# The last five tiles of a weight matrix are loaded in two DMAs of unequal numbers of partitions

## The chip, the cores and the metric

The kernel runs on one core of one Trainium2 chip. The metric is the device time of one execution in microseconds (us), as the median of several runs. The core has the engines PE (TensorE, matrix products), DVE (VectorE), ACT (ScalarE), POOL (GpSimd) and SP (SyncE, which here only issues DMAs), and 16 DMA engines that all DMAs of the core share.

## What is computed

One layer of a diffusion backbone over 512 latent tokens of width 1024 with 256 context tokens. First comes a token mixer (a bidirectional state-space scan and a gated short convolution between two projections), then an expert-retrieval mixer. The second part holds most of the time. Cut to what matters:

```python
q = (xb @ w_q).reshape(T, PEER_HEADS, 2, PEER_HALF)          # w_q: 1024 x 2048
s = jnp.einsum('thpd,hpnd->thpn', q, keys)
sv, si = lax.top_k(s, PEER_TOPK)                             # 16 of 128, per head and side
cand = (sv[:, :, 0, :, None] + sv[:, :, 1, None, :]).reshape(...)
cv, ci = lax.top_k(cand, PEER_TOPK)                          # 16 experts for each of 8 heads
eid = i1 * PEER_N_KEYS + i2                                  # which expert rows
g = jax.nn.softmax(cv, axis=-1)
u = jnp.take(u_tab, eid, axis=0)
act = jax.nn.gelu(jnp.einsum('thkd,td->thk', u, xb))
return jnp.einsum('thk,thkd->td', g * act, jnp.take(v_tab, eid, axis=0))
```

Each token fetches 8 x 16 = 128 rows of u and v. They lie side by side in one table, so that a row is 2048 numbers of 4 bytes, 8 KB.

## The kernel before

Tokens lie on the 128 partitions, in four tiles. For each tile there are 128 gathers: one gather fetches, for every one of the 128 tokens of the tile, the row of one of its experts, 128 rows of 8 KB. That makes 512 gathers, numbered 0 to 511, all issued by POOL at L766 as indirect DMAs. They land in slots of SBUF of 8 KB per partition. The number of slots changes over the program, between 6 and 11, since slots come and go with the memory that other stages free. A gather waits until the gather that used its slot before is consumed.

Of each row, DVE multiplies the u half with the token and sums (L1960). ACT makes the gate (L1423, L1428). The v half times its gate is added up either by DVE (L1977) or by PE with a diagonal matrix that ACT makes (L1436, L1133). Two gathers are handled as a pair. After the last pair of a token tile ACT copies PE's sums out (L1443), and DVE adds, normalises and adds the residual (L1988 to L1999). SP stores the tile (L637).

Scores for later tiles are computed in the same time: PE multiplies the tokens with `w_q` (L1076), transposes (L1086), multiplies with the keys (L1095), and DVE ranks.

All large weights come in tiles of 128 partitions x 2048 numbers (8 KB per partition, 1 MB) through a ring of four buffers, `wring`. SP issues their loads in one written order, the list `loads`; load n goes into buffer n % 4, after the last user of load n - 4 is through. Each buffer has a semaphore, to which every load adds 16 when it has landed, and PE waits for the right multiple of 16 in `weights(n)`. The tiles of `w_q` are loaded twice, eight for token tiles 0 and 1, and from `wq_0[1]` on eight more for token tiles 2 and 3. These last eight are the last weights of the program. Here they are called tile 0 to tile 7. PE's products take them in pairs (0, 1), (2, 3), (4, 5), (6, 7), each pair for two token tiles.

SP's list holds 92 DMAs in all: 1 of 128 rows of vectors, 80 weight tiles with 128 rows of 8 KB each, 6 token tiles of 128 rows, 1 that loads 256 rows of tokens again and 4 stores of 128 rows. ACT issues eight: one of 104 rows (`rows_b`), the dt weights and three vectors spread over 128 partitions (4 x 128), one store of 32 rows (`row_scratch`) and two loads that spread those over 128 partitions (2 x 128).

Of the kernel before, what the change touches and what calls it, by code (L numbers as in the profile page):

```python
# [19 lines left out]
P = 128  # L20
# [9 lines left out]
def build(nc, x, ctx_in, rows_a, rows_b, w_ada, w_in, w_dt, conv_w, dt_bias, a_log, d_skip, w_out, w_q, keys,  # L30
# [23 lines left out]
    WRING = 4  # L54
# [134 lines left out]
    def late_pair(s):  # L189
        return 25 + s + s // 3  # L190
# [9 lines left out]
    p = late_pair(7) + 3  # L200
# [5 lines left out]
    for n, (kind, ct) in enumerate(projs):  # L206
        product(8 + n, ("proj", n))
        p = late_pair(8 + n)
# [11 lines left out]
    for i in range(16):  # L220
        product(s + i, ("wo", i // 4, i // 2 % 2, i % 2))
        if i == 1:
            p = late_pair(s + i)
# [6 lines left out]
    p = late_pair(s + 15) + 3  # L230
# [111 lines left out]
    with ExitStack() as stack:  # L342
# [3 lines left out]
        def sem(name):  # L346
            return stack.enter_context(nc.semaphore(name))
# [4 lines left out]
        def at(kib, *dims):  # L352
            n = 1
            for d in dims:
                n *= d
            lo = int(kib * KB)
            v = arena[:, lo:lo + n]
            if len(dims) == 1:
                return v
            names = "abcd"[:len(dims)]  # L360
            return v.rearrange(f"p ({' '.join(names)}) -> p {' '.join(names)}", **dict(zip(names, dims)))

        wring = at(0, WRING, KD, WCOL)
# [102 lines left out]
        s_w = [sem(f"weights{i}_loaded") for i in range(WRING)]  # L466
# [74 lines left out]
        def await_filled(eng, name):  # L541
            b, n = place[name]
            eng.wait_ge(full[b], n + 1)
# [20 lines left out]
        loads, users = [], []  # L564

        def add_load(w, j, user):
            loads.append((w, j))
            users.append(user)
# [8 lines left out]
        z_0, proj_load, wo_0, wq_0 = [0, 0], {}, [0, 0], [0, 0]  # L577

        def mixer_loads(half):
            z_0[half] = len(loads)  # L580
            for n in range(D // WCOL):
                add_load(w_in, n, ("z", n, half))
            for kind, n in projs:
                if n % 2 == 0:
                    proj_load[kind, n, half] = proj_load[kind, n + 1, half] = len(loads)
                    add_load(w_in, {"gc": T_GC, "v": T_V, "gb": T_GB}[kind] + n // 2, (kind, n + 1, half))
            wo_0[half] = len(loads)
            if half == 0:
                for part in (1, 0):
                    for i in range(2):  # L590
                        add_load(w_out, part * (D // WCOL) + i, ("wa", 1, 0, part))
                return
            for n in range(D // WCOL):
                for part in range(2):
                    add_load(w_out, part * (D // WCOL) + n, ("wo", n, part, half))

        def query_loads(half):
            wq_0[half] = len(loads)
            for n in range(2 * QB):
                last = [u for u in units if u[1] == n // 2 and u[0] in halves[half]][-1]  # L600
                add_load(w_q, n, ("q", *last))
# [2 lines left out]
        query_loads(0)  # L604
        mixer_loads(1)
        query_loads(1)

        block = stack.enter_context(nc.Block())

        @block.sync
        def _(sp):
            sp.dma_start(rowA, rows_a).then_inc(s_rows, 16)
            for n, (w, j) in enumerate(loads):
                if n == wq_0[0]:
                    await_filled(sp, ("ob", LT - 1, 1))
                    for part in (1, 0):
                        for i in range(2):
                            slot = 2 * (1 - part) + i
                            sp.dma_start(wod[slot].rearrange("p k n -> p (k n)"),  # L620
                                         w_out[part * (D // WCOL) + 2 + i]).then_inc(s_wod[slot], 16)
                if n == wq_0[1]:
                    await_filled(sp, ("ss", 1))
                    sp.dma_start(x1[1], x[0, HS:SEQ].rearrange("(m p) d -> p m d", p=P)).then_inc(s_x1B, 16)
                for m in {2: (0, 1), 3: (2, 3), 4: (4, 5)}.get(n, ()):
                    src = x[0, m * P:(m + 1) * P] if m < LT else ctx_in[0, (m - LT) * P:(m - LT + 1) * P]
                    sp.dma_start(xin[:, m], src).then_inc(s_x[m], 16)
                if n >= WRING:
                    user = users[n - WRING]
                    if isinstance(user, int):  # L630
                        sp.wait_ge(s_wused, user)
                    else:
                        await_filled(sp, user)
                sp.dma_start(wring[:, n % WRING].rearrange("p k n -> p (k n)"), w[j]).then_inc(s_w[n % WRING], 16)
            for t in range(LT):
                sp.wait_ge(s_fin, t + 1)
                sp.dma_start(out[0, t * P:(t + 1) * P, :], x1t[t]).then_inc(s_out[t // NA], 16)  # L637
            for n in range(2):
                sp.wait_ge(s_out[n], 16 * NA)
# [132 lines left out]
        def _(pe):  # L772
            mm, tr = nc.tensor.matmul, nc.tensor.transpose

            def weights(n):
                pe.wait_ge(s_w[n % WRING], 16 * (n // WRING + 1))
                return wring[:, n % WRING]

            pe.wait_ge(s_const, 1)
# [3 lines left out]
            def ada(name, first, lhs, rows_):  # L783

                ps = claim(name)
                for i in range(2):
                    w = weights(first + i)
                    for k in range(KD):
                        last = mm(ps[0:rows_, i * WCOL:(i + 1) * WCOL], lhs(k), w[:, k, :],  # L789
                                  start=(k == 0), stop=(k == KD - 1))  # L790
                    if i == 0:
                        last.then_inc(s_wused, 1)
                filled(last, name)
# [52 lines left out]
            for n in range(XBC // WCOL):  # L846
                w = weights(xbc_0 + n)
# [18 lines left out]
            def z_part(hq, half, i):  # L866
                name = ("z", hq, half)
                ps = claim(name) if i == 0 else bank_of(name)
                w = weights(z_0[half] + hq)
                for k in range(KD):  # L870
                    last = mm(ps[:, i * WCOL:(i + 1) * WCOL], hT_tile(halves[half][i], k), w[:, k, :],  # L871
                              start=(k == 0), stop=(k == KD - 1))
                if i:
                    filled(last, name)
# [42 lines left out]
            def proj(n, half=0):  # L917
                name = (*projs[n], half)
                project_T(name, weights(proj_load[name]), name[1] % 2, lambda k: hTl[:, half, k, :])
# [58 lines left out]
            def y_transpose(m):  # L978
                pe.wait_ge(s_yn, m + 1)
                src = zs[:, m] if m < NA else yB[:, m - NA]  # L980
                for h in range(2):
                    ps = claim(("yT", m, h))
                    for k in range(4):
# [3 lines left out]
            parts = {"proj": proj, "step": step, "cb": c_times_b, "r": decay_sums, "y": diagonal, "off": entering,  # L987
                     "yT": y_transpose}
# [4 lines left out]
            def sum_squares(half):  # L993
                ps = claim(("ss", half))
                if half:
                    pe.wait_ge(s_sqaB, NX)
                else:
                    pe.wait_ge(s_sqa, NX)
                for i in range(NA):
                    last = mm(ps[:, i:i + 1], sqacc[half][:, i * P:(i + 1) * P], ones[:, 0:1], start=True, stop=True)  # L1000
                filled(last, ("ss", half))
# [37 lines left out]
            def wo_part(nq, part, i, half):  # L1039
                name = ("wo", nq, part, half)  # L1040
                if i == 0:
                    ps = claim(name)
                    if part == 0 and nq == 0:
                        for m in halves[half]:
                            for h in range(2):
                                await_read(pe, ("yT", m, h))
                    if part == 1 and nq == 0 and half:
                        pe.wait_ge(s_scB, NX)
                else:
                    ps = bank_of(name)  # L1050
                w = weights(wo_0[half] + 2 * nq + part)
                for k in range(KD):
                    src = scT[half][:, k, i * P:(i + 1) * P] if part else yT_tile(halves[half][i], k)
                    last = mm(ps[:, i * WCOL:(i + 1) * WCOL], src, w[:, k, :], start=(k == 0), stop=(k == KD - 1))  # L1054
                if i:
                    filled(last, name)
# [87 lines left out]
            def add_rows(j):  # L1144
                for n in (2 * j, 2 * j + 1):
                    if by_pe(n):
                        add_row(n)

            parts = {"h2T": queries_T, "q": query_half, "qT": query_T, "s": scores, "pk": add_rows,
                     "q0": first_query, "qT0": first_query_T, "s0": first_scores, "wa": wo_early,  # L1150
                     "z": lambda hq, i: z_part(hq, 1, i), "proj": lambda n: proj(n, 1), "yT": y_transpose,
                     "ss": lambda: sum_squares(1), "wo": lambda nq, part, i: wo_part(nq, part, i, 1)}
# [916 lines left out]
```

## Time and profile before

| | |
|---|---|
| median of 3 runs | 1911.65 us (1911.55 to 1912.14) |
| the profiled execution | 1912.31 us |
| its span, first to last instruction | 1910.6 us |
| DVE busy | 1476.7 us (77%) |
| PE busy | 1455.4 us (76%) |
| POOL busy | 895.5 us (47%) |
| DMA queue 0 (POOL's gathers and loads) | 555.78 MB, 70.6% of 16 engines' span |
| DMA queue 1 (SP) | 90.25 MB, 12.0% |

Times in the trace count from the span's start. The profiler tells of each DMA queue how many packets it moved in a stretch, and of all 16 DMA engines together the share of the time in which they were busy and the GB/s that they moved. It does not say which DMA engine moved a packet. A share slightly over 1 means that all of them were busy throughout.

### The profile page before, as it was taken

The page shows a single profiled execution, that of the slowest core. Times are in us where ns is not written, and L with a number is a line of the kernel's source. Part 1 is how long each engine was busy: PE and PEld are TensorE (multiplying, and loading weights), DVE is VectorE, ACT ScalarE, POOL GpSimd, SP SyncE. Part 2 cuts the span into 40 slices and gives each one's busy share as a digit, 9 for nine tenths or more (in the row PEclk, how much of TensorE's full clock was granted, in tenths as well). Part 3 has the DMA queues.
Part 4 walks back from the last instruction along what each step waited for, and adds up shares of the span by engine and source line. Part 5 has one row for each costly group of instructions (what it writes and reads, how often), then busy time and mean ns, then how long its engine had stood idle before and what let it go on. Part 6 is the DMA issues. An engine that isn't in the chain of part 4 may idle for free.

```text
span 1910.6 us, 15790 instructions
## 1 busy us (share of the span) xinstructions
PE 1455.4 (76%) x4607; PEld 848.5 (44%) x4607; DVE 1476.7 (77%) x2802; ACT 509.0 (27%) x1428; POOL 895.5 (47%) x658
## 2 busy tenths in 40 slices
PE   8999998999878787877778687767755655565554
PEld 4565587878645554555455244434311111111111
DVE  1645359993696778988977788889888889988876
ACT  3200120112332244222412432233322222222222
POOL 0778513330354444543434355446655555555551
PEclk9999999999989989999888798879888677868776
DMA  8434311235699999999999999999999999999994
GB/s 327 163 131 155 111 67 66 88 115 217 272 391 420 422 421 414 422 421 421 421 420 421 397 396 422 422 422 421 421 421 422 422 421 422 421 422 422 421 422 196
DMA packets 90940, 650.43 MB, mean 340 GB/s; under 512 B 10462, under 2 KB 10854, under 8 KB 12646
## 3 DMA queue, kind: packets, MB, share of 16 engines
q0 software_dynamic: 76448, 555.78, 70.6%
q1 hardware_dynamic: 13376, 90.25, 12.0%
q10 hardware_dynamic: 1029, 3.39, 0.5%
q8 instruction: 38, 0.62, 0.1%
q14 instruction: 49, 0.39, 0.1%
HBM read 647.26 MB, written 2.11 MB: 340 GB/s over the span
## 4 chain that ended last, share of the span: by engine, by line
DMA 40%; PE 30%; DVE 20%; issue 6%; ACT 3%; POOL 1%; SPq 0%; DVEq 0%; POOLq 0%; ACTq 0%
DMA arena<-in_peer_uv,arena 40%; PE bank L834 12%; DVE arena L1960 7%; PE bank L1133 6%; DVE arena L1977 4%; PE bank L1023 3%; PE bank L789 2%; PE bank L871 1%; POOL arena L766 1%; PE bank L1076 1%; PE bank L948 1%; ACT arena L1428 1%; DVE arena L1924 1%; ACT smalls L1436 1%; DVE arena L1722 1%
## 5 line engine op out<-in xcount | busy, mean ns | idle before, releaser
L766 POOL DMA_INDIRECT arena<-in_peer_uv,arena x512 | 697.0, 1361 | 740.8 <-DVE arena L1977 436.4
L1133 PE MATMUL bank<-arena,smalls 128*128 128x512 f32 x1056 | 672.3, 773 | 419.7 <-ACT smalls L1436 416.8
L1960 DVE CUSTOM_DVE_ANT_0 arena<-arena 128x1024 f32<-128x1024 f32 x512 | 619.5, 1223 | 161.3 <-DMA arena<-in_peer_uv,arena 157.9
L1133 PEld LDWEIGHTS bank<-arena,smalls 128*128 128x128 f32 x1056 | 224.6, 231 | 788.9 <-ACT smalls L1436 584.5
L1977 DVE SCALAR_TENSOR_TENSOR arena<-arena 128x1024 f32<-128x1024 f32 x244 | 311.8, 1278 | 36.2 <-ACT arena L1428 33.4
L834 PE MATMUL bank<-arena 128*128 128x256 f32 (+1 forms) x1216 | 333.7, 431 | 4.2 <-ACT arena L1198 3.7
L1423 ACT ACTIVATE arena<-arena 128x2 f32<-128x2 f32 x256 | 52.1, 203 | 928.3 <-DVE arena L1960 928.2
L834 PEld LDWEIGHTS bank<-arena 128*128 128x128 f32 x1216 | 234.3, 194 | 103.9 <-issue 78.1
L1428 ACT ACTIVATE arena<-arena 128x1 f32<-128x1 f32 x512 | 123.0, 287 | 8.4
L1076 PE MATMUL bank<-arena 128*128 128x256 f32 x480 | 109.9, 382 | 0.0
L1436 ACT ACTIVATE smalls<-ident,arena 128x128 f32<-128x128 f32 x264 | 105.1, 401 | 8.4
L1076 PEld LDWEIGHTS bank<-arena 128*128 128x128 f32 x480 | 92.4, 193 | 24.9 <-issue 13.7
L721 POOL TENSOR_TENSOR arena<-early,smalls 128x512 f32<-128x512 f32 x32 | 40.5, 1287 | 83.4 <-PE bank L948 55.3
L1579 DVE TENSOR_SCALAR arena<-bank,early 128x512 f32<-128x512 f32 (+1 forms) x28 | 18.4, 692 | 71.8 <-PE bank L834 71.8
L673 POOL TENSOR_TENSOR arena<-arena,cs 128x2048 f32<-128x2048 f32 x16 | 57.7, 3607 | 33.8 <-PE bank L842 27.6
L1561 DVE SCALAR_TENSOR_TENSOR arena<-bank,early,arena 128x496 f32<-128x496 f32 (+1 forms) x112 | 62.6, 622 | 0.6
L1054 PE MATMUL bank<-arena 128*128 128x256 f32 x256 | 61.3, 394 | 0.3 <-DVE arena L1781 0.3
L1054 PEld LDWEIGHTS bank<-arena 128*128 128x128 f32 x256 | 51.7, 202 | 17.8 <-issue 11.1
L871 PE MATMUL bank<-arena 128*128 128x256 f32 x256 | 58.3, 386 | 0.0
L1023 PE MATMUL bank<-arena 128*128 128x256 f32 x256 | 56.0, 379 | 0.0
L871 PEld LDWEIGHTS bank<-arena 128*128 128x128 f32 x256 | 49.5, 195 | 10.3 <-issue 3.8
L1023 PEld LDWEIGHTS bank<-arena 128*128 128x128 f32 x256 | 48.4, 190 | 6.5
(259 smaller groups left out, 1288.3 us busy)
## 6 DMA issues: line engine op xcount, KB each, us to landing
arena<-in_w_in SPq DMA_DIRECT2D x40, 1024.0 KB
arena<-in_w_ada POOLq DMA_DIRECT2D x16, 1024.0 KB, 5.2
arena<-in_w_out SPq DMA_DIRECT2D x16, 1024.0 KB, 12.6
arena<-in_peer_w_q SPq DMA_DIRECT2D x16, 1024.0 KB
arena<-in_w_ada SPq DMA_DIRECT2D x8, 1024.0 KB
arena<-in_peer_uv,arena POOLq DMA_INDIRECT x512, 23.8
arena<-in_x SPq DMA_DIRECT2D x4, 512.0 KB, 12.1
arena<-row_scratch ACTq DMA_DIRECT2D x1, 2048.0 KB, 9.6
```

The lines of the kernel that those rows point to most:

```text
L766: nc.gpsimd.indirect_dma_start(gslot[slot], None, uv_tab[0], bass.IndirectOffsetOnAxis(eid[t % 2][:, k:k + 1], 0)).then_inc(s_gsl[slot], 16)
L834: last = mm(dst, w[:, k, j * P:(j + 1) * P], hT(k), start=(k == 0), stop=(k == KD - 1))
L871: last = mm(ps[:, i * WCOL:(i + 1) * WCOL], hT_tile(halves[half][i], k), w[:, k, :], start=(k == 0), stop=(k == KD - 1))
L1023: last = mm(ps[:, i * WCOL:(i + 1) * WCOL], src, w[:, k, :], start=(k == 0), stop=(k == KD - 1))
L1054: last = mm(ps[:, i * WCOL:(i + 1) * WCOL], src, w[:, k, :], start=(k == 0), stop=(k == KD - 1))
L1076: last = mm(ps[:, i * WCOL:(i + 1) * WCOL], h2T[:, m % NA, k, :], w[:, k, :], start=(k == 0), stop=(k == KD - 1))
L1133: last = mm(acc[h][:, :], diag[:, k % NDG], row_v(n)[:, h * 512:(h + 1) * 512], start=first, stop=last_one)
L1428: A(wexp[:, k + i:k + i + 1], gate[t % 2][:, k + i:k + i + 1], ACT.Copy, scale=gelu[:, k + i:k + i + 1]).then_inc(s_wexp, 1)
L1436: A(diag[:, r % NDG], ident[:], ACT.Copy, scale=wexp[:, k + i:k + i + 1]).then_inc(s_diag, 1)
L1561: return V.scalar_tensor_tensor(out=d, in0=s, scalar=w, in1=d, op0=ALU.mult, op1=ALU.add)
L1960: V.tensor_tensor_reduce(row_u(n), row_u(n), h2[t], 1.0, 0.0, ALU.mult, ALU.add, dots[:, k:k + 1]).then_inc(s_dot, 1)
L1977: V.scalar_tensor_tensor(out=vacc, in0=row_v(n), scalar=w, in1=vacc, op0=ALU.mult, op1=ALU.add).then_inc(s_vadd, 1)
```

## The change

Of the eight last tiles of `w_q`, tiles 3 to 7 are loaded by two DMAs each in place of one: the first 120, 126, 117, 108 and 121 partitions, and then the remaining 8, 2, 11, 20 and 7. Both DMAs add 16 to the buffer's semaphore. PE's wait counts the transfers of the buffer so far. Bytes, source, target and order stay as they are.

```diff
+        first_part = {wq_0[1] + 3 + i: parts for i, parts in enumerate((120, 126, 117, 108, 121))}
+        transfers = [1 + (n in first_part) for n in range(len(loads))]
...
-                sp.dma_start(wring[:, n % WRING].rearrange("p k n -> p (k n)"), w[j]).then_inc(s_w[n % WRING], 16)
+                tile, cut = wring[:, n % WRING].rearrange("p k n -> p (k n)"), first_part.get(n, P)
+                sp.dma_start(tile[0:cut], w[j, 0:cut]).then_inc(s_w[n % WRING], 16)
+                if cut < P:
+                    sp.dma_start(tile[cut:P], w[j, cut:P]).then_inc(s_w[n % WRING], 16)
...
             def weights(n):
-                pe.wait_ge(s_w[n % WRING], 16 * (n // WRING + 1))
+                pe.wait_ge(s_w[n % WRING], 16 * sum(transfers[n % WRING:n + 1:WRING]))
                 return wring[:, n % WRING]
```

The end of SP's program before, from tile 0 of the last eight on (`in_peer_w_q` is `w_q`; `bank..._full` tells SP that PE's products with the buffer's previous tile are done; the last DMA row is the four stores):

```order
L634 DMA arena<-in_peer_w_q 128x2048 [waits bank0_full]
L634 DMA arena<-in_peer_w_q 128x2048 [waits bank1_full]
L634 DMA arena<-in_peer_w_q 128x2048 [waits bank2_full]
L634 DMA arena<-in_peer_w_q 128x2048 [waits bank3_full]
L634 DMA arena<-in_peer_w_q 128x2048 [waits bank2_full] x2
L634 DMA arena<-in_peer_w_q 128x2048 [waits bank1_full] x2
L637 DMA out<-arena 128x1024 [waits out_ready] x4
```

The same place of SP's program after the change, from tile 3 on:

```order
L637 DMA arena<-in_peer_w_q 120x2048 [waits bank3_full]
L639 DMA arena<-in_peer_w_q 8x2048
L637 DMA arena<-in_peer_w_q 126x2048 [waits bank2_full]
L639 DMA arena<-in_peer_w_q 2x2048
L637 DMA arena<-in_peer_w_q 117x2048 [waits bank2_full]
L639 DMA arena<-in_peer_w_q 11x2048
L637 DMA arena<-in_peer_w_q 108x2048 [waits bank1_full]
L639 DMA arena<-in_peer_w_q 20x2048
L637 DMA arena<-in_peer_w_q 121x2048 [waits bank1_full]
L639 DMA arena<-in_peer_w_q 7x2048
L642 DMA out<-arena 128x1024 [waits out_ready] x4
```

The waits stand where they stood, at the first part of each tile; the second part follows at once. No other engine's instructions change but for their line numbers.

## Rows read from the trace of the kernel before

**Rows 1.** The page: span; packets, MB and share by DMA queue

```profile
span 1910.6 us, 15790 instructions
...
q0 software_dynamic: 76448, 555.78, 70.6%
q1 hardware_dynamic: 13376, 90.25, 12.0%
q10 hardware_dynamic: 1029, 3.39, 0.5%
q8 instruction: 38, 0.62, 0.1%
q14 instruction: 49, 0.39, 0.1%
```

**Rows 2.** Windows (stretch: its us, busy us by engine, PEclk, DMA share, GB/s)

```profile
1150.00:1200.00 50.00, 38.73 (x120) 22.44 (x120) 42.95 (x94) 12.90 (x44) 26.48 (x20) 0.89 1.01 421
1600.00:1650.00 50.00, 28.21 (x40) 9.12 (x40) 47.83 (x96) 13.83 (x45) 28.94 (x20) 0.78 1.01 422
```

**Rows 3.** Windows at the end (columns: PE, PEld, DVE, ACT, POOL, PEclk, share, GB/s)

```profile
1880.00:1882.00 2.00, 0.93 (x2) 0.00 (x0) 1.27 (x3) 0.57 (x3) 0.00 (x0) 0.60 0.98 410
...
1883.00:1884.00 1.00, 1.00 (x4) 0.38 (x2) 1.00 (x2) 0.00 (x0) 0.00 (x0) 1.00 0.28 115
...
1885.00:1886.00 1.00, 0.00 (x0) 0.00 (x0) 0.93 (x1) 0.00 (x0) 0.00 (x0) 1.00 0.12 49
...
1887.00:1888.00 1.00, 0.46 (x1) 0.30 (x2) 1.00 (x1) 0.45 (x2) 0.00 (x0) 1.00 0.08 33
1888.00:1889.00 1.00, 1.00 (x3) 0.53 (x2) 1.00 (x2) 0.00 (x0) 0.00 (x0) 0.71 0.06 25
1893.00:1895.00 2.00, 2.00 (x3) 0.67 (x2) 1.34 (x4) 0.00 (x0) 0.00 (x0) 0.50 0.04 16
```

**Rows 4.** DMA queues from 1888 to 1895 us

```profile
q0 software_dynamic: 23, 0.16, 5.6%
```

**Rows 5.** The chain that ended last, its end (start, us, what)

```profile
1871.53 23.36 DMA arena<-in_peer_uv,arena
...
1894.91 0.04 DVE arena L1960
```

**Rows 6.** Timelines of SP and PE, single windows: loads of the last tiles, their first uses

```profile
1053.07 0.33 SPq L634 DMA_DIRECT2D arena<-in_peer_w_q  x1
...
1200.83 0.80 SPq L634 DMA_DIRECT2D arena<-in_peer_w_q  x2
...
1234.00 0.80 SPq L634 DMA_DIRECT2D arena<-in_peer_w_q  x2
...
1234.85 45.64 SPq L637 DMA_DIRECT2D out<-arena  x2
...
1166.44 0.38 PE L1076 MATMUL bank<-arena 128*128 128x256 f32 x1
...
1294.67 3.62 PE L1076 MATMUL bank<-arena 128*128 128x256 f32 x16
```

**Rows 7.** Windows with a DMA share under 1, and the chain there

```profile
1075.00:1080.00 5.00, 5.00 (x12) 2.31 (x11) 4.23 (x10) 2.52 (x7) 2.41 (x2) 0.90 0.68 234
1075.00:1115.00 40.00, 32.85 (x64) 12.86 (x63) 34.27 (x70) 15.89 (x46) 16.54 (x15) 0.86 0.93 361
...
1070.98 13.22 DMA arena<-in_peer_uv,arena
...
1090.67 14.77 DMA arena<-in_peer_uv,arena
...
1110.20 10.30 DMA arena<-in_peer_uv,arena
```

**Rows 8.** Landings: gathers issued from 1255 to 1300; one in the chain at 508

```profile
DMA to landing us min/median/max: 12.8/12.8/12.8
...
508.78 7.22 DMA arena<-in_peer_uv,arena
```

## What the change was expected to do

> **What bounds the kernel now.** I read the page first, then the DMA share over the span, then the last 40 us, then the one earlier place where DMA was not full. The page [rows 1] has 556 MB on queue 0 in 76,448 packets, nearly all of it the 512 gathers of expert rows. From 1150 us on, each of the 14 stretches of 50 us to 1850 has a DMA share of 1.01 at 421 or 422 GB/s, while the busiest other engine, DVE, has at most 48 us of work in 50 (two of them in [rows 2]): DMA is the bound, and it stays full until the gathers run out. Sixteen engines at 422 GB/s are 26.4 GB/s each, so one packet of 8 KB (one partition's row) costs an engine **0.31 us**, and a gather gives each engine 8 of them, 2.5 us.
>
> The end is what the argument hangs on [rows 3]. The traffic does not stop at once: 410 GB/s to 1882, 115 in the us before 1884, then falling by steps, 49 in that before 1886, 33 in that before 1888, and from 1888 on 25 GB/s, a share of 0.06: exactly one engine of sixteen. In the window from 1888 on 23 gather packets are still to come [rows 4]. So nearly all engines are through by about 1884.0, a second one at about 1887.4 (33 GB/s in its last us is one engine and a quarter), and one works alone until about 1894.5 (four more packets after 1893, 32 KB; DVE starts on them at 1894.91). A gather counts as landed only when its last engine is, so DVE waits for that one: in the chain [rows 5] the last gather, issued at 1871.53, lands at 1894.89, and dot product, gelu, PE's last four matmuls, norm and the store follow, 15.7 us to the end at 1910.6. All gathers carry the same 8 rows per engine; what makes one engine 10.5 us late after 800 us of full traffic is something of its own. Queues 8 and 14, instruction packets [rows 1], are the only small traffic that isn't shared out in the same way.
>
> **The change part by part.** Nothing moves on PE, DVE, ACT or POOL; SP issues five more DMAs, and PE's weight waits count 32 instead of 16 for five tiles.
>
> *How rows fall on engines.* Each row of a tile is one packet, and each participating engine adds one 4-byte packet. Queue 1 confirms it: SP issues 92 DMAs with 11,904 rows, 92 x 16 = 1,472 more make 13,376 [rows 1]. Queue 10 tells what happens where 16 does not divide the rows. ACT's eight DMAs carry 904 rows; 1,029 - 904 = 125 is 7 x 16 + 13. The 104-row load ran on 13 engines, 8 rows each. Two rules fit 13: the largest divisor up to 16, or shares of 8. I take the divisor. The parts then run on 15 + 8, 14 + 2, 13 + 11, 12 + 10 and 11 + 7 engines. The Trainium skill, "DMA: Bandwidth & Descriptors", section on why a DMA increments its semaphore by 16, says the same (largest k up to 16 that divides), and that on SP's path these are always the lowest-numbered k; no row here shows the latter. If the left-out engines are always from the same end, the shares of the 640 rows, 40 an engine before, become: 0, 8, 17, 26, 35 for the five at that end, 47, 49, 49, 50, five times 51, and 52, 52. In time: -12.4 us for the outermost engine, -9.9, -7.1, -4.3, -1.6, and +2.2 to +3.7 us for the eleven others.
>
> *Where these rows count.* Tile 3 is issued at 1053, tiles 4 and 5 at 1200.8, tiles 6 and 7 at 1234.0 [rows 6]. The last four lie in full traffic, where an engine's rows add up to the end: -9.9 us for both outer engines, +2.8 to +3.4 for nearly all loaded ones (9 to 11 rows more).
>
> Tile 3 lies ahead of a stretch where DMA is not full [rows 7]: 0.68 in 1075 to 1080, over 1075 to 1115 it is 0.93 against 1.01, 3.2 us idle per engine in all, while the chain goes landing (13.2, 14.8, 10.3 us), dot product, PE, next issue. There the late engine sets the landings; 8 rows less on it are 2.5 us, and what the chain gains there all engines gain. Bounds 0 (DVE, 34.3 us busy of these 40, takes it) and 2.5; I take **1.5**, nearer the chain, since each of its turns passes through a landing.
>
> *Does the relieved engine keep its 9.9 us?* Only while it has work queued. The landing in 1255 to 1300 is 12.8 us after the issue; a gather issued into nearly empty queues took 7.2 [rows 8]. So at least 5.6 of the 9.9 are kept, and at most all.
>
> *The sum, if the late engine is one of the outer ones.* It ends at 1894.5 - 1.5 - 5.6 = 1887.4 or before. The mass: 1884.0 + 3.4 - 1.5 = 1885.9. The second-latest, if loaded: 1887.4 + 2.8 - 1.5 = **1888.7**, and it is the last now. The end moves by 1888.7 - 1894.5 = **-5.8 us**. The profiled execution took 1912.31 (span 1910.6 [rows 1] and 1.7 around it), 0.7 above the median 1911.65: 1912.3 - 5.8 = 1906.5, as a median 1905.8.
>
> *Costed at nothing.* Five more issues on SP, 0.33 us for one and 0.80 for two [rows 6]: behind them stand tile issues and the first store of outputs; whoever waits for stores waits for the second, issued 45 us later [rows 6]. Later landing of uneven tiles: at most 12 rows instead of 8 on one engine, 1.2 us, doubled beside gathers; PE uses tile 3 at 1166, 113 us after its issue, and tile 6 at 1295, 61 us after its own [rows 6]; tiles 4, 5 and 7 stand alike. If that cover were gone PE's query, and with it the ranking, would be some 2.5 us late each time. A rule speaks against the change: the same page's rules for kernel authors say to use one 128-partition transfer and all 16 engines. By it the split gains nothing and costs issue time, 0 to 2 us; rows 3 say that using all engines evenly is just what leaves one late.
>
> **The rivals.**
> 1. *The late engine is among the eleven loaded ones.* Slower: it gets 8 to 12 rows more, +2.5 to +3.7 us, 1914.2 to 1915.4. For it: no view numbers the engines, and by count eleven of sixteen are loaded. By that rule the two late ones [rows 3] are these two; 15 is the outermost and 7 a loaded one, so the forecast needs 15 to be the later; the other way round gives +3.1 us, 1914.8.
> 2. *Both late engines are outer ones.* Then the mass is last: 1885.9, or with tile 3's full 2.5 us 1884.9: -8.6 to -9.6, 1903.1 to 1902.1.
> 3. *The late one is only slightly relieved* (4.3 or 1.6 us): 1907.3 to 1910.
> 4. *Rows fall in shares of 8.* Then each short part lies on one to three engines at the start of the row; the first gets +33 rows, 25 of them after 1200: 7.8 us more than 1884.0 is 1891.8, a gain of 2.7 at best, 1909, and queue 1 would count 13,380 packets.
> 5. *It does nothing*: the gathers balance the engines again within the slots. Against: engines stay busy after 1150 and the lateness survives to the end [rows 2, 3]. 1911.7.
>
> **How the numbers follow.** Forecast 0.52; both outer 0.12; slightly relieved 0.05; late engine loaded 0.23; shares of 8 or no effect 0.08 together. The likeliest own range is 1904 to 1908 (tile 3 from 0 to 2.5, 1 us either way for reading the ends). The loaded case holds more than 0.2, so the whole range must reach it: 1902.3 to 1915.5. A measurement of this kernel can tell 0.2%, 3.8 us. Faster by more: 0.52 + 0.12 and half of the third, less a little for a forecast that falls short: 0.65. Slower by more: the loaded case peaks at 3.7 us, just under the line, so only a third of it and some mishap: 0.11. Same: 0.24.
>
> **What the changed profile would show.** Queue 1 with 13,376 - 80 + 103 = 13,399 packets (the divisor rule). The lone-engine tail: traffic of all engines until about 1885, then no long stretch at 25 GB/s, last landing near 1889. Share still 1.01 after 1150. The idle in 1075 to 1105 shorter. Rival 1 would show a lone tail of 10 us still, all of it 3 us later; rival 2 a tail under 2 us. What would make it wrong above all: the number of the late engine, which I choose and don't read.

## The result: 1.2% slower, and the profile after

| | before | after |
|---|---|---|
| median of the runs | 1911.6 us (4 runs, 1909.21 to 1912.14) | 1933.5 us (4 runs, 1930.55 to 1935.89) |
| the profiled execution | 1912.31 us | 1930.55 us |
| its span | 1910.6 us | 1928.8 us |
| queue 1 | 13,376 packets | 13,399 packets |

The ratio is 1.012, with a 95% interval of 1.0108 to 1.0133: 22 us slower. The two profiled executions lie 18.2 us apart, since that of before took a little longer than its four runs and that of after is the shortest of its own. All sums below go by these 18.2 us. One of the ten runs of experiment 9 took 2044 us at a granted clock of 0.705, where the other nine had 0.87 to 0.88, and counts in no ratio.

The page of the kernel after: span, DMA share and GB/s in 40 slices of 48 us, and the queues that answer to [rows 1].

```profile
span 1928.8 us, 15795 instructions
...
DMA  8433311234799999999999999999999999999994
GB/s 329 157 143 141 110 66 66 90 145 180 312 387 421 422 421 421 421 421 420 422 420 402 377 417 420 353 345 419 421 422 421 421 421 422 422 421 421 422 421 203
...
q0 software_dynamic: 76448, 555.78, 70.6%
q1 hardware_dynamic: 13399, 90.25, 12.2%
```

The two lines have to be read against each other. The DMA line is 9 in every slice from 530 us to the last but one: the engines are busy throughout, as before. The GB/s line has two dips in that stretch, 402 and 377 (1013 to 1109 us) and 353 and 345 (1206 to 1302 us). The first covers the load of tile 3, the second those of tiles 4 to 7. (The kernel before has a dip at the first place too, to 397 and 396, but there the share is below 1 [rows 7].) A busy share that stays full while the GB/s fall says that each packet takes longer.

Windows of 50 us of the kernel before (columns as in [rows 2]):

```profile
1050.00:1100.00 50.00, 33.13 (x66) 13.72 (x65) 39.09 (x85) 22.16 (x57) 18.16 (x16) 0.79 0.98 398
1100.00:1150.00 50.00, 39.77 (x110) 20.55 (x109) 44.19 (x77) 17.55 (x52) 29.10 (x22) 0.91 0.98 397
1200.00:1250.00 50.00, 32.11 (x87) 17.33 (x86) 37.53 (x77) 14.12 (x40) 20.57 (x17) 0.83 1.01 422
1250.00:1300.00 50.00, 36.69 (x107) 20.39 (x107) 45.68 (x86) 15.97 (x45) 26.34 (x18) 0.79 1.01 422
1300.00:1350.00 50.00, 35.42 (x113) 20.14 (x111) 45.27 (x95) 16.30 (x48) 33.73 (x23) 0.93 1.01 422
```

The same windows of the kernel after:

```profile
1050.00:1100.00 50.00, 29.29 (x58) 11.71 (x56) 34.74 (x78) 20.36 (x51) 15.59 (x15) 0.80 1.00 370
1100.00:1150.00 50.00, 38.31 (x108) 19.89 (x108) 44.61 (x79) 17.57 (x54) 28.44 (x21) 0.93 1.00 408
1200.00:1250.00 50.00, 30.69 (x84) 17.02 (x83) 35.67 (x74) 13.50 (x38) 19.09 (x16) 0.80 1.01 364
1250.00:1300.00 50.00, 25.77 (x73) 14.16 (x71) 32.02 (x61) 12.13 (x32) 16.61 (x14) 0.74 0.98 339
1300.00:1350.00 50.00, 39.71 (x109) 22.12 (x108) 46.26 (x95) 16.17 (x48) 30.48 (x22) 0.78 1.01 419
```

These ten rows hold the whole loss. 50 us at 28 GB/s less is 1,400 KB, and 1,400 KB at 422 GB/s are 3.3 us. Worked out like that, the five stretches lose 3.3, -1.3, 6.9, 9.8 and 0.4 us: 19.1 us, against 18.2 in the span. Before 1050 and after 1350 nothing is lost: the other windows of 50 us between 400 and 1850 differ by 4 GB/s at most, either way.

How long one packet takes follows from the rows of the queues: share x 16 engines x the window, divided by the MB in pieces of 8,192 bytes. The kernel before, 1203 to 1223 us (queue: packets, MB, share):

```profile
q0 software_dynamic: 869, 6.33, 76.0%
q1 hardware_dynamic: 288, 2.10, 25.2%
```

The kernel after, the same stretch, in which tiles 4 and 5 land:

```profile
q0 software_dynamic: 534, 3.90, 66.2%
q1 hardware_dynamic: 293, 2.09, 35.5%
```

Before, 0.76 x 320 us over 773 rows is 0.315 us on queue 0, and 0.252 x 320 over 256 is 0.315 us on queue 1. After, they take **0.445 us** on both (0.662 x 320 over 476, 0.355 x 320 over 255). The gathers, which nothing in the change touches, pay as much per row as the loads, and there are nearly twice as many of them.

The end of the kernel after, in windows of 2 us (columns as in [rows 3]):

```profile
1900.00:1902.00 2.00, 0.00 (x0) 0.00 (x0) 1.23 (x2) 0.53 (x3) 0.00 (x0) 1.00 0.66 274
1902.00:1904.00 2.00, 1.36 (x2) 0.84 (x3) 2.00 (x2) 0.55 (x2) 0.00 (x0) 0.63 0.19 78
...
1906.00:1908.00 2.00, 0.69 (x2) 0.30 (x2) 1.40 (x3) 1.08 (x4) 0.00 (x0) 1.00 0.07 29
1910.00:1912.00 2.00, 0.00 (x0) 0.00 (x0) 1.38 (x3) 0.68 (x3) 0.00 (x0) 1.00 0.06 25
1912.00:1914.00 2.00, 1.51 (x2) 0.63 (x3) 2.00 (x2) 0.41 (x2) 0.00 (x0) 0.69 0.07 29
```

The tail of one engine at a share of 0.06 is still there, from about 1907 to 1914.9, where DVE starts on the last landing:

```profile
1914.95 1.23 DVE L1965 CUSTOM_DVE_ANT_0 arena<-arena 128x1024 f32<-128x1024 f32 x1 [0.66 <-DMA arena<-in_peer_uv,arena]
```

In [rows 5] that was 1894.91, 20.0 us earlier. Of these 20.0 us, 18.6 are the traffic as a whole (the last gather's landing on the median engine moved from 1883.7 to 1902.3) and 1.4 the last engine, which is further behind (12.6 us for 11.2). What follows took 1.8 us less this time (13.9 for 15.7).

### The profile page after: what moved, and what is told of

It is laid out like the page before. It is cut to its first block, busy times and chain, and to the rows that moved or that the text cites. A ratio compares the mean times of both kernels' runs of the same rounds, so it can differ in the third digit from the quotient of the medians.

```text
span 1928.8 us, 15795 instructions
## 1 busy us (share of the span) xinstructions
PE 1455.6 (75%) x4607; PEld 847.5 (44%) x4607; DVE 1477.4 (77%) x2802; ACT 508.9 (26%) x1428; POOL 900.4 (47%) x658
## 3 DMA queue, kind: packets, MB, share of 16 engines
q1 hardware_dynamic: 13399, 90.25, 12.2%
## 4 chain that ended last, share of the span: by engine, by line
DMA 43%; PE 27%; DVE 19%; issue 6%; ACT 3%; POOL 1%; SPq 0%; DVEq 0%; POOLq 0%; ACTq 0%
DMA arena<-in_peer_uv,arena 43%; PE bank L839 11%; DVE arena L1965 6%; PE bank L1138 4%; DVE arena L1982 4%; PE bank L1028 3%; PE bank L794 2%; PE bank L876 1%; POOL arena L771 1%; PE bank L953 1%; DVE arena L1929 1%; ACT arena L1433 1%; DVE arena L1727 1%; PE bank L965 1%; PE bank L815 1%
## 5 line engine op out<-in xcount | busy, mean ns | idle before, releaser
L1059 PEld LDWEIGHTS bank<-arena 128*128 128x128 f32 x256 | 50.9, 199 | 17.2 <-issue 10.9
L876 PEld LDWEIGHTS bank<-arena 128*128 128x128 f32 x256 | 49.6, 195 | 10.3 <-issue 3.8
```

## Experiments

Eleven kernels ran. The first question was which part of the change costs: the second DMA, the engines left out, or where the rows go. Each time is a median, each ratio one to the kernel before on the same chip, whose medians were 1910.2 to 1911.0 us. A ratio rests on all runs of both kernels and can differ a little from that of the two medians.

**1. Two DMAs a tile, each of all 128 partitions and half the columns.** Same count of DMAs and waits, all engines alike.

```diff
-                sp.dma_start(tile[0:cut], w[j, 0:cut]).then_inc(s_w[n % WRING], 16)
                 if cut < P:
-                    sp.dma_start(tile[cut:P], w[j, cut:P]).then_inc(s_w[n % WRING], 16)
+                    sp.dma_start(tile[:, 0:half], w[j][:, 0:half]).then_inc(s_w[n % WRING], 16)
+                    sp.dma_start(tile[:, half:], w[j][:, half:]).then_inc(s_w[n % WRING], 16)
```

Expected: 

> The five tiles are again loaded in two DMAs each, but cut by columns: both parts have all 128 partitions and half the numbers of each row. Theory PLACEMENT (an uneven number of partitions makes DMA engines write partitions that others write too, and all packets beside it grow): no cut of partitions, so packets stay at 0.31 us per 8 KB (0.16 for 4 KB), traffic stays at 421 GB/s in 1200 to 1250 us, time 1911 to 1913 us. Theory TWO DMAS (a second DMA per tile costs by itself): about the changed kernel's 1933 us. Theory FEW ENGINES (the parts run on 15 to 2 engines and these get more rows): 1911 to 1912 us, as all 16 take part.

Measured: 1909.72 us (10 runs), ratio 1.0001 (0.9992 to 1.0011). More issues, more packets, a semaphore that counts to 32: all of it costs nothing that can be measured.

**2. Cuts at 112 + 16 and 3. at 64 + 64.** Both parts divide by 16, so every engine gets exactly its 8 rows of each tile.

```diff
-        first_part = {wq_0[1] + 3 + i: parts for i, parts in enumerate((120, 126, 117, 108, 121))}
+        first_part = {wq_0[1] + 3 + i: parts for i, parts in enumerate((112, 112, 112, 112, 112))}      # 2
+        first_part = {wq_0[1] + 3 + i: parts for i, parts in enumerate((64, 64, 64, 64, 64))}           # 3
```

Expected of 112 + 16: 

> The five tiles are cut in 112 + 16 partitions: 16 divides both, so every engine carries 7 + 1 = 8 rows as before, and queue 1 has 13,376 + 80 = 13,456 packets. Theory PLACEMENT: seven rows in a row for each engine do not match the places that the gathers use; packets grow to 0.45 us or so during the loads and the time is 1920 to 1935 us. Theory FEW ENGINES: shares are even, 1911 to 1913 us. Theory TWO DMAS: about 1933 us.

Expected of 64 + 64: 

> The five tiles are cut in 64 + 64 partitions, 4 + 4 rows on each of 16 engines. Theory PLACEMENT: each half reaches half of the places at which DMA can write (by the Trainium skill's page SBUF - State Buffer, section on the DMA port swizzle, partitions 0 to 63 have 8 of 16 ports), so two engines share each, packets of both queues near 0.5 to 0.6 us during the loads, 1920 to 1940 us. Theory FEW ENGINES: even shares, 1911 to 1913 us.

Measured: 1928.36 us, 1.0086 (1.0069 to 1.0103), and 1929.41 us, 1.0095 (1.0078 to 1.0112). The queues of 64 + 64 over the 10 us from 1204.8:

```profile
q0 software_dynamic: 253, 1.82, 61.9%
q1 hardware_dynamic: 137, 0.99, 40.3%
```

By the same division a gather's row takes 0.446 us and a load's 0.534. The shares of the engines are as even as in the kernel before, and still 16 and 18 of the 22 us are lost. So the main part of the loss is not due to the uneven shares, on which the whole prediction was built, but to the partitions to which each engine writes. (Which rows of the source it reads changes with them; experiment 4 tells the two apart.)

**4. The loads alone.** No layer is computed: the kernel clears 128 x 32,768 numbers of SBUF and then loads one group of rows after the other, each group waited for before the next, the loads of one group to places that don't overlap. It ran once, in 386.28 us. The first nine groups are eight tiles each, cut to their first 128, 120, 126, 117, 108, 121, 112, 96 and 64 partitions. Then come groups of four DMAs of 16 partitions with 32 KB for each partition, 256 packets of 8 KB in all: to 16 neighbouring partitions, to every 4th, to every 8th, and the first and the last of these again with every 8th row of the source.

```python
for sem, group in zip(sems, loads):
    for dst, src in group:
        sp.dma_start(dst, src).then_inc(sem, 16)
    sp.wait_ge(sem, 16 * len(group))
```

Expected: 

> All work is left out but loads by SP and the four stores: fourteen stretches one after the other, each of 8 loads of 8 KB rows with 128, 120, 126, 117, 108, 121, 112, 96 and 64 partitions, and then five stretches of 4 loads that fill 16 partitions with 4 rows of 8 KB each: partitions 0 to 15, every fourth from 0, every eighth from 0 with the same source rows 0 to 15, and then partitions 0 to 15 and every eighth with source rows 0, 8, 16 and so on. No gathers are beside them. Theory PLACEMENT, on the side of the target: 128 rows at 420 GB/s with packets of 0.31 us; the others clearly slower than their engines allow, packets of 0.4 to 0.6 us; 16 neighbouring partitions slowest (packets over 1 us, near 105 GB/s), every fourth and every eighth about 210 GB/s, whatever the source rows. Theory FEW ENGINES: packets 0.31 us everywhere, GB/s as 16, 15, 14, 13, 12, 11, 16, 16 and 16 engines of 26.4 each: 422, 396, 369, 343, 317, 290, 422, 422, 422, and 422 for the last five. A theory of the source's side: the stretches that differ in the source rows alone differ.

The windows of this kernel, one for each group in the order above (stretch, its us, DVE, POOL, clock, DMA share, GB/s):

```profile
36.10:56.80 20.70, 0.00 (x0) 0.00 (x0) 1.00 0.96 404
58.30:96.20 37.90, 0.00 (x0) 0.00 (x0) 1.00 0.92 206
97.80:121.10 23.30, 0.00 (x0) 0.00 (x0) 1.00 0.86 353
122.50:147.00 24.50, 0.00 (x0) 0.00 (x0) 1.00 0.80 313
148.40:173.40 25.00, 0.00 (x0) 0.00 (x0) 1.00 0.74 283
174.70:218.70 44.00, 0.00 (x0) 0.00 (x0) 1.00 0.68 180
220.20:246.40 26.20, 0.00 (x0) 0.00 (x0) 1.00 0.97 279
248.00:274.00 26.00, 0.00 (x0) 0.00 (x0) 1.00 0.97 241
275.80:296.30 20.50, 0.00 (x0) 0.00 (x0) 1.00 0.99 203
298.10:316.60 18.50, 0.00 (x0) 0.00 (x0) 1.00 1.00 113
319.50:330.50 11.00, 0.00 (x0) 0.00 (x0) 1.00 0.92 191
332.30:342.60 10.30, 0.00 (x0) 0.00 (x0) 1.00 0.99 204
344.60:363.70 19.10, 0.00 (x0) 0.00 (x0) 1.00 0.96 109
366.00:376.80 10.80, 0.00 (x0) 0.00 (x0) 1.00 0.93 193
```

Two things are read here. The share times 16 counts the engines: 120 partitions 14.7 (of 15), 126 13.8 (of 14), 117 12.8 (of 13), 108 11.8 (of 12), 121 10.9 (of 11). That is the largest divisor up to 16 each time. And 16 x share x 8.192 over the GB/s is the time of a packet: 0.31 us for 128 partitions, 0.59 for 120, 0.32 for 126, 0.34 for 117 and 108, 0.50 for 121, 0.46 for 112, 0.53 for 96, 0.64 for 64. With the same 16 engines, 16 neighbouring partitions take nearly twice as long as 16 that lie 8 apart (113 and 204 GB/s), and the rows of the source hardly matter (113 and 109, 204 and 193). The placement theory holds here, except that it expected 0.4 to 0.6 us for 126, 117 and 108 as well.

The Trainium skill, "SBUF — State Buffer", section on Door 1, the DMA port swizzle, has a rule for this: a transfer reaches SBUF by 16 ports of 8 partitions each, bits 2 to 4 and bit 6 of the partition number pick the port, 16 neighbouring partitions reach 4 ports and partitions 0 to 63 reach 8. It gives 104 GB/s for partitions 0 to 15 and 196 for 0 to 63; the runs here have 113 and 203, so the trace agrees.

Sixteen engines are slow or quick by where their rows fall. In a whole tile, says the Trainium skill in "DMA: Bandwidth & Descriptors", section "The descriptor swizzle", each engine writes to 8 partitions that are just one port, its own; the first group's 404 GB/s agrees. 120 partitions on 15 engines ran at half of 128's rate. That fits runs of 8 neighbouring partitions for each engine, so that two engines are always at one port; runs of 9 on 14, 13 or 12 engines shift against each other, and alone they are nearly free. That the parts are dealt out in runs is inferred from these rates; no view names an engine's partitions. The inference can be put to the test by working the nine groups through row by row, as an estimate: engines that write to one port at a time share it, an engine alone takes 0.31 us, the parts go out in runs, and the ports are those of the Trainium skill's rule above. In the order of the groups this gives 0.31, 0.62, 0.31, 0.31, 0.31, 0.57, 0.50, 0.59 and 0.62 us, within 0.08 us of every measured value.

**5. The same cuts on five `w_in` tiles near the program's start**, issued between 37 and 102 us, where the DMA engines are not the bound: a window of this kernel.

```diff
-        first_part = {wq_0[1] + 3 + i: parts for i, parts in enumerate((120, 126, 117, 108, 121))}
+        first_part = {xbc_0 + 1 + i: parts for i, parts in enumerate((120, 126, 117, 108, 121))}
```

```profile
30.00:110.00 80.00, 74.12 (x294) 42.39 (x294) 41.73 (x59) 16.54 (x30) 43.15 (x26) 0.98 0.55 173
```

Expected: 

> The same cuts (120, 126, 117, 108, 121) on five tiles at the start of the program, loads 9 to 13, where the traffic is 110 to 160 GB/s and PE sets the pace; tiles 3 to 7 of the last eight are whole again. Theory PLACEMENT: the packets grow there too, but nothing waits for DMA: 1909 to 1913 us. Theory that the cut costs something on the issuing or waiting engines: a few us more, 1913 to 1933 us.

Measured: 1912.17 us, 1.0011 (1.0002 to 1.0021). With a share of 0.55 the same cuts cost some 2 us for the five tiles in place of 22. This stretch differs from the late one in two things, engines that are not full and no gathers beside the loads; the run does not tell which of them spares the cost.

**6. All five tiles 120 + 8**, a cut that halved the rate in experiment 4.

```diff
-        first_part = {wq_0[1] + 3 + i: parts for i, parts in enumerate((120, 126, 117, 108, 121))}
+        first_part = {wq_0[1] + 3 + i: parts for i, parts in enumerate((120, 120, 120, 120, 120))}
```

Expected: 

> All five tiles are cut in 120 + 8, the size that ran at 207 GB/s by itself. Shares of rows: one engine 0 of 40, seven 40, eight 45. Theory PLACEMENT: five stretches of some 9 us at about 255 GB/s where 421 were to be had, 3.7 us each, 1926 to 1931 us. The theory of my forecast (shares of rows decide): eight engines 1.6 us later, one relieved by 12.4 us: 1905 to 1912 us.

Measured: 1934.05 us, 1.0114 (1.0097 to 1.0131), 3 us above the range of the placement theory and about the change itself. Alone, 126, 117 and 108 were nearly free and 120 was not; beside gathers there is no such difference.

**7. Half of each tile, at the engines' own places, and 8. the same half in one DMA.** Both kernels load only partitions 0 to 63 of tiles 3 to 7 and leave the rest out, so PE multiplies with old numbers there. In 7 there are eight DMAs of 8 partitions each, spaced so that, by the port rule above, their eight engines write to one port each; in 8 there is one DMA.

```diff
+                    for c in (0, 1, 2, 3, 32, 33, 34, 35):      # 7
+                        sp.dma_start(tile[c:c + 29:4], w[j, c:c + 29:4]).then_inc(s_w[n % WRING], 16)
...
+                    sp.dma_start(tile[0:64], w[j, 0:64]).then_inc(s_w[n % WRING], 16)      # 8
```

Expected of 7: 

> Of tiles 3 to 7 only partitions 0 to 63 are loaded (64 to 127 keep what the buffer held, the products with them are not the reference's). They come in 8 DMAs of 8 partitions each, every fourth one (0, 4, ... 28, then 1, 5, ... and 32, 36, ...): 8 engines with 8 rows each, and by the rule of the whole tile each on the partitions that it writes in a gather as well. Theory PLACEMENT: packets stay at 0.31 us and the traffic at 421 GB/s; the eight engines have as many rows as before, so 1909 to 1911 us if the late engine is one of them, down to 1903 us if it is not. Theory FEW ENGINES or theory MORE DMAS (eight for each tile): 1915 us or more.

Expected of 8: 

> Of tiles 3 to 7 only partitions 0 to 63 are loaded (the rest as in the run with aligned parts), in one DMA of 64 partitions: 16 engines with 4 rows each. Theory PLACEMENT: packets near 0.55 us, 250 GB/s for some 4 us a tile; that loses 1.7 us a tile, and 20 rows less on each engine give back 6.2 us in all: 1911 to 1914 us. Theory FEW ENGINES: only the 6.2 us count, 1904 us, less than with aligned parts on eight engines.

Measured: 1911.0 us, 1.0001 (0.9991 to 1.0011), and 1914.86 us, 1.0018 (1.0008 to 1.0027). The queues of 7 from 1203 to 1223, and behind them a window of 8 while a load lands:

```profile
q0 software_dynamic: 1014, 7.37, 91.1%
q1 hardware_dynamic: 207, 0.83, 10.1%
```

```profile
1205.00:1215.00 10.00, 5.01 (x12) 2.20 (x12) 7.22 (x11) 1.57 (x5) 2.75 (x3) 0.80 1.02 276
```

In 7 a gather's row takes 0.324 us and a load's 0.319, although the eight engines of the load do double duty. The even half in one DMA over all 16 engines would spare every engine 20 rows in five tiles, 6.3 us, if rows cost 0.314 us; it lost 3.4 instead. So the placement costs, with bytes and engine shares even, some 10 us for half the bytes.

**9. As 7, but seven partitions in each DMA**, so that the eighth engine of the lower half is left out as well (partitions 28 to 31 and 60 to 63 are left out with it).

```diff
-                        sp.dma_start(tile[c:c + 29:4], w[j, c:c + 29:4]).then_inc(s_w[n % WRING], 16)
+                        sp.dma_start(tile[c:c + 25:4], w[j, c:c + 25:4]).then_inc(s_w[n % WRING], 16)
```

Expected: 

> As the run with the lower 64 partitions in aligned parts, but each part has 7 partitions instead of 8 (0, 4, ... 24 and so on), so that partitions 28 to 31 and 60 to 63 are left out as well, and the eighth engine of the lower half gets none of the 40 rows. Question: is the late engine that one? The Trainium skill, page DMA: Bandwidth & Descriptors, section on latency and other measured facts, says engines 7 and 15 are usually slower. If it is: it has 12.4 us less work, of which at least 5.6 are kept, and the lone tail of some 7 us at the end shrinks to 0 to 2 us: 1903 to 1906 us. If it is another one: 1909 to 1912 us, as with eight.

Measured: 1910.89 us, 1.0000 (0.9990 to 1.0010). These two kernels show in which half the late engine is. A gather's 16 landings, one for each engine, can be picked out of the trace by their semaphore; here worked out for the gather number in front (counted from 0), in us against their median:

```
7, gather 258   -3.2 -3.2 -3.2 -3.1 -2.8 -2.7 -2.3 -2.2   2.2  2.6  2.6  2.8  3.3  3.3  4.5  9.6
9, gather 258   -0.5 -0.4 -0.4 -0.4 -0.4 -0.3 -0.3 -0.2  0.2   5.0  5.1  5.2  7.1  8.1  8.2 11.9
after, g. 263  -10.1 -9.7 -9.3 -7.7 -5.2  -1.0 -0.3 -0.2  0.2  0.3  0.6  0.7  1.6  2.0  2.0  5.1
after, g. 269   -1.1 -1.0 -1.0 -1.0 -0.9 -0.9 -0.3 -0.2  0.2  0.3  0.6  0.7  1.6  1.9  2.0  5.1
```

In 7 eight engines are ahead and eight behind, and the late one, 5 us behind the next, is among the loaded eight. In 9 nine are ahead and seven behind, and it is among the seven. In the kernel after five engines are ahead, those with few rows, and the late one is not among them. So in all three it is a loaded one.

**10. Only tile 3 cut (120 + 8), and 11. only tiles 6 and 7 cut (108 + 20, 121 + 7).**

```diff
-        first_part = {wq_0[1] + 3 + i: parts for i, parts in enumerate((120, 126, 117, 108, 121))}
+        first_part = {wq_0[1] + 3 + i: parts for i, parts in enumerate((120,))}          # 10
+        first_part = {wq_0[1] + 6 + i: parts for i, parts in enumerate((108, 121))}      # 11
```

Expected of 10: 

> Only tile 3 is cut, in 120 + 8; tiles 4 to 7 are whole. It is issued at 1053 us, ahead of the stretch in which DMA was idle for 3.2 us of 40. Theory PLACEMENT: 9.3 us at 254 GB/s lose 3.7 us, and what the idle can take of it is back: 1911 to 1914 us. The forecast's step (8 rows less for the late engine are 1.5 us gained): 1908 to 1909 us.

Expected of 11: 

> Only tiles 6 and 7 are cut, into 108 + 20 and 121 + 7 as in the change; tiles 3 to 5 are whole. Theory of crossed places: in the profile after the change, 1246.9 to 1269.6 ran at 262 GB/s where 421 were due, 22.7 x (1 - 262/421) = 8.6 us, and nothing else is lost: about +8 to +9 us, 1919, with the stretch after 1234 at 250 to 290 GB/s and tiles 3 to 5 at 421. Together with tile 3 alone (+5.0) that leaves about +8 for tiles 4 and 5. Rival, one delay once: whichever cut comes first upsets the order of the slots and costs most of the 22 us, so that two late tiles would cost 15 or more. Rival, only the relieved engines matter: no loss, since tiles 6 and 7 leave four or five engines out like the others.

Measured: 1915.57 us, 1.0024 (1.0013 to 1.0035), and 1920.93 us, 1.0054 (1.0041 to 1.0068). Two windows of 11, before its first cut tile and over its two:

```profile
1200.00:1230.00 30.00, 20.40 (x49) 10.68 (x48) 25.71 (x49) 9.36 (x26) 14.15 (x11) 0.72 1.01 422
1234.00:1260.00 26.00, 8.54 (x19) 3.20 (x17) 12.24 (x24) 4.85 (x13) 7.74 (x6) 0.77 1.02 300
```

Tiles 4 and 5, whole in 11, land at 422 GB/s where the kernel after has 364. Tiles 6 and 7 cost 10.3 us (1.0054), where 8 to 9 had been expected from a window said to run at 262 GB/s; the trace has 274 there. The windows of the kernel after put 10.2 us on these two tiles and 6.9 on tiles 4 and 5, which were not cut alone. Tile 3 costs 4.6 us alone (1.0024; the median is 1.6 us above the expected range), and in the change as a whole its stretch lost 2.0. One late tile does not upset all that follow. No experiment gave a version that beats the kernel before.

## Why the prediction was wrong

It said 1905.8 us, between 1902.3 and 1915.5, and slower with a chance of 0.11. The time came 18 us above the upper end, so no rival held it either.

*How rows fall on engines*: the divisor rule was right. Queue 1 has its 13,399 packets, and experiment 4 counts the engines one cut at a time. Which engines are left out stands in no row.

*What a row costs*: this is the step that failed. That a packet of 8 KB costs an engine 0.31 us was read from a kernel in which every full-height transfer gives every engine its own partitions, and the sum then used it for parts that deal them out in another way ("in full traffic, where an engine's rows add up to the end"). The runs showed 0.445 us in the stretch of tiles 4 and 5, on queue 0 as on queue 1, and that is the whole of the result: 19.1 us of traffic lost by the windows. What settles it is two sets of tests: with the shares even, by columns 1.0001, 112 + 16 1.0086, 64 + 64 1.0095; with half the bytes, at the engines' own places 1.0001, in one DMA 1.0018, although that one spares every engine rows.

*Where these rows count*: the stretches were right and the sign wrong. Tile 3 was to gain 1.5 us and costs 4.6 by itself. Its stretch had only 3.2 us idle per engine [rows 7] to hide a loss in. In the change as a whole the windows from 1050 to 1150 lose 3.3 us and give 1.3 back; in experiment 10 they run at 378 GB/s on average where before has 398, which is 4.7 us.

*Which engine is late*: the forecast chose an outer one and priced a loaded one as the slower rival. The runs say loaded. With rows at 0.31 us that would have meant +2.5 to +3.7 us; it did not decide here. The late engine's lag behind the median was 11.2 us at the last gather before and 12.6 after. Nor had this lag grown over "800 us of full traffic". In the kernel before it was 8.6 us at gather 165 (986 us), 2.1 at gather 208, behind the stretch with a share below 1, and 7.0 at gather 255 (1238); at gather 264 (1267) it was back at 3.4.

*Does a relieved engine keep its gain?* "At least 5.6 of the 9.9 are kept" failed too. At gather 263 five engines were 5 to 10 us ahead, at gather 269, about 15 us later, none was more than 1.1. Gather 264, issued 10.4 us after 263, lands on these five within 0.3 us of each other: all of them had been waiting for it. An engine that is ahead runs out of issued gathers, because the next one waits for a slot, and that for the last engine's landing. The window 1250 to 1300 shows it: a share of 0.98 in place of 1.01 is 0.03 x 50 x 16 = 24 us of one engine, 5 for each of five. Kernel 7 shows it too: at gather 258 a gap of 4.4 us lies between the eight leading engines and the other eight, at gather 268, 30 us later, one of 0.4. This is the balancing within the slots that rival 5 had named and the prediction had turned down. A relieved late engine could therefore have saved about the 3.4 us that it was behind at gather 264, since the rest of its 11.2 came later (an estimate from these landings). The 5.6 us came from a landing of 12.8 us against one of 7.2 [rows 8]; that the queues hold 5.6 us of work says how far an engine can run ahead for one gather, not that the lead lasts 600 us.

*Costed at nothing*: right. SP's issues took 0.27 to 0.41 us each, and the trace of after has no idle time of PE before the query's matmuls. The rule of the Trainium skill against the change ("DMA: Bandwidth & Descriptors", "Rules for kernel authors": use one 128-partition transfer) pointed the right way. The reason that it gives is that the two halves share the same engines anyway, and the prediction had priced that at 0 to 2 us; the measured loss is 22 us.

Left open: why one engine is late at all. It falls behind by about 1 us in 75 while the traffic is full (3.4 us at 1298, 11.2 at the end, from the landings of before), and it is one of the seven that experiment 9 loads; that the instruction packets of queues 8 and 14 do it was argued and not tested. Open too is why 126, 117 and 108, nearly free alone, cost as much as 120 beside gathers. A load that writes to the ports of other engines while these write gathers there would do it, and kernel 7 fits that. The estimate of experiment 4, with each engine taking gather rows and load rows in turn, gives 271 GB/s for 120 + 8 and 303 for 126 + 2 and 117 + 11, so nearly the same loss for both kinds; the windows have 283 (experiment 6, 1204 to 1224) and 288. But no run separates this from other causes.

## What to carry to other kernels

Before a full-height tile is cut along partitions, ask to which partitions each DMA engine will write: a cut along the columns kept every engine at its own place and was free, a cut along the partitions cost 3.3 to 5.2 us a tile while the DMA engines were full with gathers, and 2 us for five tiles where their share was 0.55 and no gathers ran. Where the DMA share stays at 1.0, read the GB/s beside it and work out the time of a packet for each queue: a transfer can slow down the others without any wait appearing. A load taken off some DMA engines doesn't help when all transfers wait for the last engine and few are in flight.

## What was not expected of the hardware

- Two loads of 1 MB, each cut in two parts, slowed the gathers beside them by 41% per row (0.315 to 0.445 us), on another queue and issued by another engine.
- 120 partitions alone ran at 206 GB/s and 126 at 353, with 15 and 14 engines.
- The seven or eight engines that are loaded at their own places (kernels 9 and 7) take the load at 0.32 us a row, beside full gathers; the two queues of kernel 7 moved 8.2 MB in 20 us, 410 GB/s, and the time is unchanged (1.0001).
- Five engines can be 5 to 10 us ahead of the rest and within about 1 us of it 15 us later.
